# One flow step on one Trainium2 core: all tiles of three projections keep their split weights, normalised tiles are prepared without GpSimd, norm sums move by a unit

## The reference: what is computed

```python
def rms_norm(x, g):
    y = xf * lax.rsqrt(jnp.mean(xf * xf, axis=-1, keepdims=True) + EPS)
    return (y * g.astype(jnp.float32)).astype(x.dtype)

def modulate(x, g, shift, scale):
    return rms_norm(x, g) * (1 + scale[:, None, :]) + shift[:, None, :]

def gated_residual(x, y, g, gate):
    return x + gate[:, None, :] * rms_norm(y, g)

def channel_mixer(h, w1, w2):
    return jnp.square(jax.nn.relu(h @ w1)) @ w2
```

## Time and profile before

| | us |
|---|---|
| three runs, median (lowest to highest) | 1907.51 (1906.75 to 1907.51) |
| the profiled execution: its own time | 1910.7 |
| its span, first to last instruction | 1908.9 |
| PE busy / DVE busy / ACT busy / POOL busy | 1773.7 / 1104.3 / 716.7 / 290.6 |
| mean granted TensorE clock | 0.956 |

### The profile page before, as it was taken

The page is one execution under the profiler, slowest core; times in us unless marked ns, Lnnn a source line. Parts: engine busy times, 40 slices in busy tenths (PEclk is TensorE's granted clock), DMA queues, the critical chain, the costliest instruction groups (busy, mean ns, idle before and its releaser), DMA issues.

```text
span 1908.9 us, 27129 instructions
## 1 busy us (share of the span) xinstructions
PE 1773.7 (93%) x10964; PEld 1559.0 (82%) x10964; DVE 1104.3 (58%) x1749; ACT 716.7 (38%) x1196; POOL 290.6 (15%) x300
## 2 busy tenths in 40 slices
PE   7799997779899999999978998999899999999997
PEld 3599872358899999999978886333789999999997
DVE  2567836763666777776466655556466563333345
ACT  1323215364554322312333464565345432131232
POOL 2300000142420000000143030333241100000012
PEclk9799998899999999999987998999989999999998
DMA  8354322102336546455330030000334552222231
GB/s 269 99 167 154 111 66 66 34 1 67 111 110 201 153 143 187 134 161 148 100 86 18 18 108 1 1 1 1 89 89 122 166 155 78 68 77 78 78 89 56
DMA packets 271806, 184.18 MB, mean 96 GB/s; under 512 B 13005, under 2 KB 246338, under 8 KB 271682
## 3 DMA queue, kind: packets, MB, share of 16 engines
q1 hardware_dynamic: 271682, 182.44, 32.7%
HBM read 178.87 MB, written 3.62 MB: 96 GB/s over the span
## 4 chain that ended last, share of the span: by engine, by line
PE 77%; DVE 9%; ACT 5%; issue 4%; POOL 3%; DMA 2%; SPq 0%; ACTq 0%; DVEq 0%; POOLq 0%
PE ps L734 20%; PE ps L736 19%; PE ps L735 19%; PE ps L1253 3%; PE ps L805 2%; PE ps L1263 1%; POOL rstd L2406 1%; ACT w_hi L520 1%; DMA stage<-in_w_mlp_out 1%; PE ps L866 1%; PE ps L867 1%; PE ps L868 1%; DVE nt L1822 1%; DVE w_lo L529 1%; PE ps L749 1%
## 5 line engine op out<-in xcount | busy, mean ns | idle before, releaser
L520 ACT ACTIVATE w_hi<-stage 128x1024 fp32r<-128x1024 f32 (+1 forms) x189 | 198.2, 1051 | 714.5 <-PE ps L736 560.3
L529 DVE TENSOR_TENSOR w_lo<-stage,w_hi 128x1024 fp32r<-128x1024 f32 (+1 forms) x189 | 236.8, 1256 | 379.5 <-ACT w_hi L520 379.0
L734 PE MATMUL ps<-hM_hi,w_lo 128*128 128x320 f32 x984 | 310.4, 315 | 13.2 <-POOL hM_lo L2410 12.9
L735 PE MATMUL ps<-hM_lo,w_hi 128*128 128x320 f32 x984 | 307.2, 312 | 0.0
L736 PE MATMUL ps<-hM_hi,w_hi 128*128 128x320 f32 x984 | 307.1, 312 | 0.0
L734 PE MATMUL ps<-h_hi,w_lo 128*128 128x320 f32 x872 | 271.0, 311 | 3.7 <-DVE h_lo L2199 2.6
L736 PE MATMUL ps<-h_hi,w_hi 128*128 128x320 f32 x872 | 269.4, 309 | 0.0
L735 PE MATMUL ps<-h_lo,w_hi 128*128 128x320 f32 x872 | 269.4, 309 | 0.0
L2406 POOL TENSOR_TENSOR rstd<-rstd,sq 128x320 f32<-128x320 f32 x98 | 99.9, 1025 | 960.2 <-ACT sq L1342 957.6
L734 PEld LDWEIGHTS ps<-hM_hi,w_lo 128*128 128x128 f32 x984 | 187.6, 191 | 20.0 <-POOL hM_lo L2410 16.6
L735 PEld LDWEIGHTS ps<-hM_lo,w_hi 128*128 128x128 f32 x984 | 187.6, 191 | 0.0
(11 more groups left out here) (344 smaller groups left out, 3471.7 us busy)
## 6 DMA issues: line engine op xcount, KB each, us to landing
stage<-in_w_mlp_out SPq DMA_DIRECT2D x86, 512.0 KB, 4.3
stage<-in_w_mlp_in SPq DMA_DIRECT2D x80, 512.0 KB, 4.2
slab_mlp<-in_w_ada SPq DMA_DIRECT2D x28, 1024.0 KB, 5.4
stage<-in_w_in_ac SPq DMA_DIRECT2D x28, 512.0 KB, 3.8
slab_ac<-in_w_ada SPq DMA_DIRECT2D x12, 1024.0 KB, 6.2
ada_a<-in_w_ada SPq DMA_DIRECT2D x8, 1024.0 KB, 8.1
stage<-in_w_out_ac SPq DMA_DIRECT2D x11, 512.0 KB, 4.4
stage<-in_w_out_c SPq DMA_DIRECT2D x11, 512.0 KB, 4.2
```

The source lines that it names most:

```text
L520: nc.scalar.activation(hi_place(n)[:, 0:width], stage[:, n % STAGE, 0:width], ACT.Copy)\
L529: nc.vector.tensor_tensor(lo_place(n)[:, 0:width], stage[:, n % STAGE, 0:width], hi_place(n)[:, 0:width].bitcast(F32), ALU.subtract).then_ ...
L734: mm(out, lo[:, k], xh, start=j == 0, stop=False)
L735: mm(out, hi[:, k], xl, start=False, stop=False)
```

## The change

- `KEEP` becomes 8 in `out0`, `down03` and `out1`: no piece is loaded or split twice there. Five of the pieces go to new slots `wm_hi`/`wm_lo` in the first 40 KB, where `hM_hi` and `hM_lo` lie. The second sweep takes tiles 2 to 6 first, then 7, 0, 1. `split_plan` places the first pieces of `up00`, `in_c` and `up10` by hand: pieces 0 and 1 behind units 5 and 6 of the sweep stage, piece 2 behind unit 13, 3 and 4 behind units 0 and 1 of their own stage; in_c's last piece and uq's first two move behind in_c's unit 9.
- `low_part` on GpSimd is gone but for `in0`. VectorE's `low` makes the low part one tile behind `modulate`. In half 0 VectorE multiplies x, coefficient and root in one instruction, ScalarE adds the shift while rounding, VectorE adds it again in the low part. In half 1 VectorE multiplies x and root, ScalarE applies scale and shift (two instructions) and rounds (a third), VectorE subtracts.
- GpSimd adds squares 1 to 5 only; TensorE sums the added tile, square 6 and square 7.
- Sums and spreads move: y's sum from tile 4 to tile 3 of its unit and its spread into the same unit at tile 7; x's sum one unit earlier (two in the half-1 stages), its spread at tile 1 of the next unit. The tables of residuals and tiles follow.
- The residual's first instruction takes the coefficient, its second is a plain add.
- GpSimd writes the constants of `kmas` and `rope` after in_c may start, and no longer adds for `cq`.

```diff
-KEEP = 5
-SECOND = {8: (3, 4, 5, 6, 7, 2, 1, 0), 6: (3, 4, 5, 2, 1, 0)}
+KEEP = {"out0": 8, "down03": 8, "in_c": 5, "out1": 8, "down13": 5}
+SECOND = {"out0": (2, 3, 4, 5, 6, 7, 0, 1), "down03": (2, 3, 4, 5, 6, 7, 0, 1), "in_c": (3, 4, 5, 2, 1, 0),
+          "out1": (2, 3, 4, 5, 6, 7, 0, 1), "down13": (3, 4, 5, 6, 7, 2, 1, 0)}
...
+            if KEEP.get(name) == 8 and j >= 2:
+                slot = KEPT_IN[j - 2]
+            if name == "in_c" and j == k - 1:
+                slot = slots[PIECE_AT[name] + 2]
...
+            if name in AFTER_ALL and j < 5:
+                at = max(at, UNIT_AT[name] + (-11, -10, -3, 0, 1)[j])
...
+KEPT_IN = (5, 6, 7, 8, 9, 2)
+AFTER_ALL = ("up00", "in_c", "up10")
...
-RES8, MOD8 = {1: (0, 1), 2: (2, 3), 3: (4, 5), 4: (6, 7)}, {6: (0, 1, 2), 7: (3, 4, 5)}
-RES6, MOD6 = {1: (0, 1, 2), 2: (3, 4, 5), 3: (6, 7)}, {5: (0, 1, 2)}
-RES16 = {n + 1: (n,) for n in range(KD)}
-MOD16 = {11: (0,), 12: (1, 2), 13: (3, 4), 14: (5,), 15: (6, 7)}
+RES8, MOD8 = {1: (0, 1, 2), 2: (3, 4), 3: (5, 6, 7)}, {5: (0, 1), 6: (2, 3, 4), 7: (5, 6, 7)}
+RES6, MOD6 = {0: (0,), 1: (1, 2, 3), 2: (4, 5), 3: (6, 7)}, {4: (0, 1), 5: (2, 3, 4), 6: (5, 6, 7)}
+RES16 = {1: (0,), 2: (1, 2), 3: (3,), 4: (4, 5), 5: (6,), 6: (7,)}
+MOD16 = {n + 8: (n,) for n in range(KD)}
...
+        wm_hi, wm_lo = lay(0, ("wm_hi", [P, 5, PIECE], F32R), ("wm_lo", [P, 5, PIECE], F32R))
...
-                if n > 2:
-                    pe.wait_ge(added[s], ADD_AT[name] + n - 2)
+                if n > 3:
+                    pe.wait_ge(added[s], ADD_AT[name] + n - 3)
                 for b, tokens in enumerate(blocks(s)):
                     mm(out[:, b:b + 1], rstd[:, tokens], ones[:, 0:1], start=b == 0, stop=False)
...
+                for k in range(max(1, n - 2), n):
+                    pe.wait_ge(sq_done[s], at + k + 1)
+                    for b, tokens in enumerate(blocks(s)):
+                        last = mm(out[:, b:b + 1], sq[:, k % 2, tokens], ones[:, 0:1], start=False,
+                                  stop=b == 2 and k == n - 1)
...
-                return {0: {4: lambda: sum_squares(y_name, s)}, 1: {0: lambda: spread_root(y_name, s)},
+                return {0: {3: lambda: sum_squares(y_name, s), 7: lambda: spread_root(y_name, s)},
                         last_sums: {6: lambda: sum_squares(x_name, s)},
-                        last_sums + 1: {4: lambda: spread_root(x_name, s)}}.get(at)
+                        last_sums + 1: {1: lambda: spread_root(x_name, s)}}.get(at)
...
+            def operand(name, s, k):
...
+                if s == 0:
+                    f(hM_hi[:, k, half(0)], place, ACT.Identity, bias=mod[:, layer, 8 * shift + k, 0:1])\
+                        .then_inc(h_hi_done[0], 1)
+                    return
+                for a, b, g in HALVES[1]:
+                    part = place[:, a - HALF:b - HALF]
+                    last = f(part, part, ACT.Identity, scale=coef[:, layer, which, k, g:g + 1],
+                             bias=mod[:, layer, 8 * shift + k, g:g + 1])
+                last.then_inc(affine_done, 1)
+                act.wait_ge(affine_done, KD * (MOD_NO[name] - 1) + k + 1)
+                f(hM_hi[:, k, half(1)], place, ACT.Copy).then_inc(h_hi_done[1], 1)
...
+            def modulate(name, s, k):
...
+                if s == 0:
+                    last = stt(place, x, coef[:, layer, which, k, 0:1], spread(name, 0), ALU.mult, ALU.mult)
+                else:
+                    last = tt(place, x, spread(name, 1), ALU.mult)
+                last.then_inc(h_full[s], 1)
+
+            def low(name, s, k):
...
+                dve.wait_ge(h_hi_done[s], KD * MOD_NO[name] + k + 1)
...
+                if s == 0:
+                    last = stt(lo, place, mod[:, layer, 8 * shift + k, 0:1], hi, ALU.add, ALU.subtract)
+                else:
+                    last = tt(lo, place, hi, ALU.subtract)
+                last.then_inc(h_lo_done[s], 1)
...
                 for k in tiles.get(at, ()):
-                    modulate(*x, s, k)
+                    modulate(x, s, k)
+                    if k:
+                        low(x, s, k - 1)
...
             def add_square(name, s, k):
 
-                if not 1 <= k <= NORM_K[name] - 2:
+                if not 1 <= k <= NORM_K[name] - 3:
                     return
```

More of the change, by code:

```diff
@@ L174 @@
 NORM_K = dict(NORMS)
[L175 removed]
+ADD_AT = {name: sum(max(0, k - 3) for _, k in NORMS[:n]) for n, (name, _) in enumerate(NORMS)}
 PIECE_AT = first_of(PIECES)
@@ L1108, in _ @@
                      ready=h_ready("in1", s) if u in (0, 6) else None,
-                     beside=beside[u] if u in beside else sums_beside("y0m", "in1", 1, 4, u))
+                     beside=beside[u] if u in beside else sums_beside("y0m", "in1", 1, 3, u))
             def latent_sums():
@@ new lines, in residual, with first_modulate @@
+                    last = stt(place[:, part], yT[:, k, a:b], coef[:, layer, which, k, g:g + 1],
+                               spread(name, s)[:, part], ALU.mult, ALU.mult)
+                link(last)
+                tt(xT[:, k, cols], xT[:, k, cols], place, ALU.add).then_inc(x_done[s], 1)
+            def first_modulate(s, k):
+                dve.wait_ge(rstd_done[s], 1)
+                if k >= 2:
+                    dve.wait_ge(h_lo_done[s], k - 1)
+                place = norm_place("in0", s, k)
+                link(tt(place, xT[:, k, half(s)], spread("in0", s), ALU.mult))
@@ L1820, in modulate @@
                 for a, b, g in HALVES[s]:
                     part = place[:, a - HALF * s:b - HALF * s]
-                    last = ts(part, part, coef[:, layer, which, k, g:g + 1],
-                              mod[:, layer, 8 * shift + k, g:g + 1], ALU.mult, ALU.add)
+                    last = ts(part, part, coef[:, 0, A1, k, g:g + 1], mod[:, 0, 8 * SHIFT1 + k, g:g + 1],
+                              ALU.mult, ALU.add)
                 last.then_inc(h_full[s], 1)
+            def modulate(name, s, k):
+                layer, which, _ = MODULATED[name]
+                dve.wait_ge(rstd_done[s], NORM_NO[name] + 1)
+                if k >= 4:
+                    dve.wait_ge(h_lo_done[s], KD * MOD_NO[name] + k - 3)
+                place, x = norm_place(name, s, k), xT[:, k, half(s)]
+                if s == 0:
[3 more added lines that the diff above has]
+                last.then_inc(h_full[s], 1)
@@ L2192, in mlp @@
                         split(name, u)
+                        if early and name[0] == "d" and u == 7:
+                            low(x, 1, KD - 1)
+                        if name == "down03" and u == 15:
+                            low("in1", 0, KD - 1)
                         if name[0] == "u":
@@ L2475, in _ @@
             pool.wait_ge(ada_red, G_MLP0 // 2)
-            pool.wait_ge(h_lo_done[0], KD * (MOD_NO["in1"] + 1))
+            pool.wait_ge(unit_done, UNIT_AT["in_c"])
+            pool.wait_ge(added[1], ADD_AT["in1"])
             nc.gpsimd.memset(kmas[96:97, :], 1.0).then_inc(km_zero, 1)
```

157 lines of the change are left out of this document (68 added, 89 removed).

## The result

| | before | after |
|---|---|---|
| median of 5 runs each, side by side (lowest to highest), us | 1907.51 (1906.75 to 1911.12) | 1897.28 (1895.09 to 1899.28) |
| ratio, with its 95% interval | | 0.9942 (0.9927 to 0.9956) |
| span of the profiled execution, us | 1908.9 | 1895.0 |

The change makes the kernel faster by 10.2 us in the medians and 13.9 us in the two spans. The forecast was a gain of 22.6 us and a time of 1885 us; the measured time lies above the range (1875 to 1897), if narrowly. The sign was right and half of the gain is missing.

A forecast was written before the change was run, and what follows sets the result against it. TensorE, busy 93% of the span, bounds the kernel; 51.8 us of its waits and half clock were reachable. Crossing gains of 23.0, less 1.0 for y1m, plus 0.6 for in0, gave 22.6 off 1907.5: 1885 us, range 1875 to 1897.

The forecast's parts named there:

- what the prediction had named as showing it wrong: Low-part waits over 1 us starting up00 or up10, or a sum in down03 or in_c still waiting 4 us.
- the price of the clock: TensorE at 1.2 GHz starts matmuls 0.267 us apart, not 0.147; one 3.4 us stretch loses 1.5 us.
- the early root in out0: Asked for at the next unit's second tile, ready 1.2 us after the unit: wait 0.8, with refill 0.95, as before.
- The low parts in in_c's second half: In in_c, the last low part is ready at 34.8 and wanted at 32.5: a wait of 2.4 us.
- three stretches of 3.4 us at 1.5 each: Half clock left after the change: 1.5 us lost each in up00/down00, in_c and up10/down10.
- In_c's sum: In in_c's second half, TensorE asks at 15.9, last square at 19.1; after two groups it waits 1.9 us.
- the lock: VectorE instructions with two SBUF inputs and GpSimd's SBUF reads exclude each other; up to 0.5 us per moved low part.
- ScalarE's three operations a tile: Half 1's normalised tiles: three ScalarE operations take some 1.1 us a tile.
- The kept weights: out0, down03 and out1 split 8 pieces, not 11, removing splits between VectorE's residuals; none stood on TensorE's path by itself.
- Early roots do not cost: Full clock behind the 2.6 us waits and in_c's half-1 tiles keep up: 1878 us, chance 0.15.
- Slower than before: 12 roots of y and x late behind ScalarE's evacuations, 2.6 idle and 1.5 half clock each: 1915 us, chance 0.06.
- In_c's second half stays bound: ScalarE's chain of three takes 1.6 us a tile, in_c loses 17: gain 13.2, 1894 us, chance 0.17.

The follow-up runs named there:

- E4: The kernel before with only the kept weights, new order of second sweeps and new split places; GpSimd still makes low parts: 1880.07 us, ratio 0.9862.
- E8: E4 with in_c's pieces 4 and 5 split behind unit 3: 1885.97 us, ratio 0.9883.
- E1: The changed kernel with x's root spread at tile 4 (half 0) or 7 (half 1), not tile 1: 1880.26 us, ratio 0.9857.
- E7: The changed kernel with ten unread 128-column matmuls ahead of the root wait in down00 and down10: 1894.95 us, ratio 0.9932.
- E12: The changed kernel, but for in_c's second-half x norm GpSimd adds 8 of 320 columns: 1892.04 us, ratio 0.9916.
- E5: The changed kernel with x's roots at tiles 4 and 7 and in_c's pieces 4 and 5 split behind unit 3: 1874.70 us, ratio 0.9828.
- E11: The changed kernel with only half 0's x roots at tile 4, half 1's left at tile 1: 1891.57 us, ratio 0.9914.

## Why the prediction was wrong

Set against the stage lengths, before less after:

| part | gain forecast | gain measured |
|---|---|---|
| out0, up00, down00, up00b | 4.9 - 3.7 = 1.2 | -0.7 |
| down03 | 1.9 | -0.9 |
| in_c | 15.4 | 4.0 |
| out1, up10, down10, up10b | 8.2 - 3.7 = 4.5 | 7.2 |
| y1m (down13) and in0 | -1.0 + 0.6 | 3.1 |

The rest of the span's 13.9 is 1.3 in down01. The misses are in_c (11.4), down03 (2.8) and out0 to down00 (1.9). Some of what was gained is luck: 2.7 of the 3.1 in the last row lie ahead of out0, where profiles of the same code differ by up to 3.0 us (E4 and E8, whose input norms are those of before, took 438.5 and 437.9 us there and before 440.1); and some 3 of the 7.2 are the stretch at out1's wait for `o`, which before has and after has not. The four rows of crossings were to give 23.0 and gave 9.6. Of what the prediction had named as showing it wrong, one came true: the sum in in_c waits 4.31 us.

**The step that failed: the price of the clock.** All waits but one were sized well: the early root in out0 was to stand 0.8 and stood 0.78; those of down00 and down10 were to stand 2.6 and did. All root waits were to be "some 10" and were 8.6. The low parts in in_c's second half were to cost 2.4 and cost 2.35 (1.44, 0.63 and 0.28); GpSimd's low-part waits vanished; out0's residuals took 8.2 us for the forecast 8. But the forecast counted the half clock after as three stretches of 3.4 us at 1.5 each, and there were 47.7 us of it. The 37.5 us on top lose up to 0.45 x 37.5 = 17 us, some 15 once the standing in them, counted as waits already, is taken off. In gains: the forecast struck out 16.2 us lost to half clock (1.5, 1.5, 3.6, 3.9, 1.5 and 4.2) and put three times 1.5 back, 11.7 us won; the time at half clock did not shrink. That alone is most of the 13.4 us missing in the crossings; in_c's sum, below, is the other large part. The error has a plain form: in the sum of what is lost now, half clock was read from the trace at every place; in the sum of what is lost after, it was assumed only behind waits of 2.6 us and once in in_c. A wait of 0.78 us in out0 came with 3.4 us of half clock (the same wait in out1 with none), those of 2.57 and 2.56 with 6.8 each; E1 removes both kinds, E7 the longer ones.

**In_c's sum.** Forecast: eight residuals of 1.1 and three splits of 1.2 end 18.6 us after down03, wait 1.9. Measured: wait 4.31. Three adds at 1.17 to 1.18 in place of 0.49 and two splits at 1.90 in place of 1.22, 0.68 x 5 = 3.4 us, is the lock that E12 takes away. The prediction did weigh the lock, and looked for it at the moved low parts alone, not at the residuals' adds, which are of the kind that is held up (two SBUF inputs, in the new form as in the old), nor at the splits.

**ScalarE's three operations a tile** took 1.33 us (0.92 for two, 0.47 for the rounding, overlapping) and not 1.1:

```profile
1021.60 0.92 ACT L1383 ACTIVATE nt<-nt,mod,coef 128x192 f32<-128x192 f32 x2
1022.55 0.47 ACT L1387 ACTIVATE hM_hi<-nt 128x320 fp32r<-128x320 f32 x1
```

Its direct cost came out as forecast, since the units give ScalarE enough time. But the three waits, 2.35 us, stand at the start of the second half-clock stretch of 10.2 us; that price was missing again.

**The kept weights** were right in their mechanism (splits stood between VectorE's residuals) and were given no price of their own. E4 shows that they give 27.8 us with the new order and places. What went with them in the change costs 17 net: the early x roots cost 17.0 (E1), and the rest, tiles without GpSimd, third group, earlier sums, comes to nothing in the sum: E1 and E4 are both at 1880. Only with both edits (E5) is the whole change ahead of the kept weights alone, by 5.4 us.

**The rivals.** "Early roots do not cost" is refuted by E1. "Slower than before" named the right mechanism, roots behind ScalarE's evacuations with half clock behind them; it asked for eight roots late by over 2 us, and two were. Those two cost 5.4 and 5.0 us by E1, more than the 4.1 it gave each; the roots of half 0 cost 5.7 together (E11). "In_c's second half stays bound" came nearest in time (1894), by a wrong cause: the tiles were not at 1.6 us each; the sum before them and the clock behind them were late.

**Still open**: what decides whether a wait of 0.8 to 3.3 us has a half-clock stretch behind it, since the same wait has one in one kernel and none in another (out1's root, the wait for `o`, down03's sum in E4 and E8). Whether it also differs between runs of one kernel is not known: there is one profile of each. A version of the changed kernel without GpSimd's squares was not tried.

## What to carry to other kernels

A short wait of TensorE is to be priced with the half-clock stretch that may come with it, on both sides of the sum: here an edit that removed 8.0 us of waits gave 17.0. Since the stretch may also stay away, a gain is better read from the lengths of the stages that an edit touches than from the whole time. Before putting a consumer earlier in an in-order queue, look at whether its producer is earlier too; if it is not, the early place only turns work into standing. Where VectorE is late, count its instructions with two SBUF inputs beside GpSimd's at their locked price, and take splits out from among them: E4, which does this, was worth more than the whole change.
